# Two weight-row stages, the head scores and the scan outputs of a two-layer mixer moved onto parts of the TensorE array

## What is computed

```
for layer in (0, 1):
    m = silu(c) @ w_mod[layer] + b_mod[layer]        # 6*1024 columns, one row for the latents, one for the context
    z = rms(x) * (1 + m[1]) + m[0]
    layer 0: p = z @ even_w_in                       # 1920 + 1024 columns
             ya = rwkv7_mix(p[:1920])                # a delta-rule scan over time, forward and backward, 8 heads of 64
             yb = rglru_mix(p[1920:])                # gates, a diagonal scan forward and backward
             y  = concat(ya, yb) @ even_w_out
    layer 1: y  = diff_attention(z) @ attn_w_o
    x = x + m[2] * y
    x = x + m[5] * peer_ffn(rms(x) * (1 + m[4]) + m[3])   # product keys, 16 experts per head gathered from HBM

step of the rwkv7 scan, per head:
    sa = state @ kk;  state = state * w - outer(sa, akk) + outer(v, k);  out = state @ r
then out (both directions) is normalised per head, scaled, gated
```

## Time and profile before

| what | value |
|---|---|
| median of 3 runs | 3483.07 us (3481.43 to 3484.12) |
| the profiled execution, its own time | 3485.71 us |
| its span, first to last instruction | 3483.9 us |
| mean granted TensorE clock | 0.933 of full speed |
| TensorE busy | 2802.4 us (80%) |
| VectorE busy | 2254.0 us (65%) |
| ScalarE busy | 701.0 us (20%) |
| POOL busy | 1090.5 us (31%) |

### The profile page before, as it was taken

The page is one execution under the profiler, slowest core; times in us unless marked ns, Lnnn a source line. Parts: engine busy times, 40 slices in busy tenths (PEclk is TensorE's granted clock), DMA queues, the critical chain, the costliest instruction groups (busy, mean ns, idle before and its releaser), DMA issues. The chain is left out here.

```text
span 3483.9 us, 31043 instructions
## 1 busy us (share of the span) xinstructions
PE 2802.4 (80%) x8972; PEld 1425.2 (41%) x8972; DVE 2254.0 (65%) x5072; ACT 701.0 (20%) x1707; POOL 1090.5 (31%) x941
## 2 busy tenths in 40 slices
PE   7697399999967999777787878787696578887777
PEld 1242288888834444322232223232344344432222
DVE  7697423332343767788887888888244367787887
ACT  2112433233102111111111111111104111111111
POOL 0010232122011444444444444444000034444443
PEclk9798699899878999999999999999899899999999
DMA  8552000000014999999999999999300189999998
GB/s 315 185 195 90 33 1 1 1 1 1 1 73 180 362 378 371 413 420 420 420 413 420 421 420 413 418 420 410 148 24 3 74 347 420 420 415 420 421 420 342
DMA packets 133878, 927.54 MB, mean 266 GB/s; under 512 B 16764, under 2 KB 17788, under 8 KB 31380
## 3 DMA queue, kind: packets, MB, share of 16 engines
q0 software_dynamic: 113472, 830.62, 58.1%
q1 hardware_dynamic: 20312, 95.72, 7.4%
HBM read 925.13 MB, written 1.15 MB: 266 GB/s over the span
## 5 line engine op out<-in xcount | busy, mean ns | idle before, releaser
L1370 PE MATMUL psum<-ring,diag 128*128 128x512 f32 x3072 | 1483.8, 622 | 374.7 <-DVE diag L1459 372.7
L1267 POOL DMA_INDIRECT ring<-in_uv,experts x768 | 914.4, 1191 | 1375.4 <-PE psum L1370 1017.9
L1481 DVE CUSTOM_DVE_ANT_0 ring<-ring,hcur 128x1024 f32<-128x1024 f32 x768 | 941.5, 1226 | 261.0 <-DMA ring<-in_uv,experts 240.2
L1370 PEld LDWEIGHTS psum<-ring,diag 128*128 128x128 f32 x3072 | 557.4, 194 | 1276.5 <-DVE diag L1459 799.4
L1301 ACT ACTIVATE gel<-dots 128x1 f32<-128x1 f32 x768 | 143.6, 201 | 1325.4 <-DVE dots L1481 1324.8
L1459 DVE TENSOR_SCALAR diag<-ident,gel,wcur 128x128 f32<-128x128 f32 x768 | 256.8, 345 | 80.2 <-ACT gel L1301 78.0
L385 PE MATMUL psum<-zT,wring 128*128 128x512 f32 x368 | 164.3, 604 | 15.7 <-DMA wring<-in_w_in 15.7
L1015 DVE COPY_PREDICATED T<-level,psum 128x512 f32<-128x512 uint32 x80 | 58.7, 734 | 180.6 <-PE psum L820 180.6
L1350 PE MATMUL psum<-hT,w_q 128*128 128x512 f32 (+3 forms) x512 | 163.1, 473 | 1.4 <-DMA w_q<-in_w_q 1.4
L1543 PE MATMUL psum<-wring,zT 128*128 128x512 f32 x320 | 140.1, 601 | 10.2 <-DMA wring<-in_w_qkv 10.2
L444 DVE SCALAR_TENSOR_TENSOR acc<-wmod,scol,acc 128x512 f32<-128x512 f32 x168 | 126.3, 752 | 6.9 <-ACT acc L411 1.2
(11 more groups left out here) (314 smaller groups left out, 2903.9 us busy)
## 6 DMA issues: line engine op xcount, KB each, us to landing
wring<-in_w_mod SPq DMA_DIRECT2D x12, 2048.0 KB, 9.7
wmod<-in_w_mod POOLq DMA_DIRECT2D x12, 2048.0 KB, 8.4
w_q<-in_w_q SPq DMA_DIRECT2D x32, 512.0 KB
ring<-in_uv,experts POOLq DMA_INDIRECT x768
wring<-in_w_qkv SPq DMA_DIRECT2D x6, 2048.0 KB, 8.4
wring<-in_w_in SPq DMA_DIRECT2D x23, 512.0 KB, 5.0
bc<-modulation_rows SPq DMA_DIRECT2D x14, 512.0 KB, 5.5
w<-in_w_out SPq DMA_DIRECT2D x8, 512.0 KB, 6.2
```

What stands on the lines that cost most here:

```text
L1267: nc.gpsimd.indirect_dma_start(ring[:, s % RING], None, uv, bass.IndirectOffsetOnAxis(ap=experts[:, n, j:j + 1], axis=0)).then_inc(row_in[ ...
L1370: m = nc.tensor.matmul(ps[:, c], diag[:, j % DIAGS], ring[:, j % RING, D + 512 * c:D + 512 * c + 512], start=(first and j == 0), stop=(las ...
L1481: nc.vector.tensor_tensor_reduce(u, u, hcur[:], 1.0, 0.0, ALU.mult, ALU.add, dots[:, j:j + 1]).then_inc(dot_done, 1)
```

## The change

`modulation`: TensorE does all 8 blocks, with 32 stationary columns of which 30 are zero (`scolz`). Block k writes PSUM partitions 32*(k % 4) to 32*(k % 4) + 31. ScalarE evacuates the bank, and one matmul against `sel` adds the four groups.

`project_even`: nothing of layer 1's modulation is left in it, but the loads of the first 4 half chunks (1 MB each), which SP issues last. Layer 1's chunks are done in `rglru` instead, 12 of them spread over its units, in a ring of 4 halves filled by SP.

`rwkv_scan`: `bF` and `kF` hold 64 real rows per head, two heads on the two row halves. Two heads' scores follow each other on the two row halves; all four products of a pair of heads go before the next pair. `R` and the outputs are made with 64 stationary columns and 128 moving ones, even heads into PSUM partitions 0 to 63, odd heads into 64 to 127, so `O` holds them turned (columns of the heads on partitions). `rwkv_finish` turns `O` back with 16 transposes before its first reduction.

```
# modulation
-    for k in range(SPLIT):
-        m = nc.tensor.matmul(ps[0:2, n % BANKS], scol[:, k], wring[:, n % RING, k], start=(k == 0), stop=False)
+    groups(nc, ps[:, n % 2], scolz, wring[:, n % RING], range(KD)).then_inc(part_mm, 1)
...
+def groups(nc, bank, scol, weight, ks):
+    for i, k in enumerate(ks):
+        g = 32 * (k % GROUPS)
+        m = nc.tensor.matmul(bank[g:g + 32], scol[:, k], weight[:, i], start=(k < GROUPS), stop=(k >= KD - GROUPS))
+    return m
...
# project_even
+                for i in range(MOD_RING):
+                    sp.dma_start(wmod[:, i], half_chunk(a, i)).then_inc(wmod_in[i], 16)
...
# rglru: SP, POOL, TensorE, ScalarE, VectorE
+        MOD_AT = lambda u: range(u + (u > 0), u + 2 if u < 7 else MOD_CHUNKS)
+                for i in range(MOD_RING, 2 * MOD_CHUNKS):
+                    sp.wait_ge(part_mm, i - MOD_RING + 1)
+                    sp.dma_start(wmod[:, i % MOD_RING], half_chunk(a, i)).then_inc(wmod_in[i % MOD_RING], 16)
...
+                for n in range(MOD_CHUNKS):
+                    if n >= 2:
+                        pool.wait_ge(row_done, n - 1)
+                    for seg in range(2):
+                        pool.dma_start(brow[seg:seg + 1, n % 2], a["b_mod"][:, 1, n * 512:(n + 1) * 512]).then_inc(b_in[n % 2], 16)
+                    if n >= 2:
+                        pool.dma_start(mod[1, :, (n - 2) * 512:(n - 1) * 512], row[:, n % 2]).then_inc(row_out[n % 2], 16)
...
+                    if u >= 1:
+                        for n in MOD_AT(u - 1):
+                            mod_groups(n)
+                for n in MOD_AT(7):
+                    mod_groups(n)
+                add_groups(MOD_CHUNKS - 1)
...
+                    for n in MOD_AT(u):
+                        act.wait_ge(part_mm, 2 * n + 2)
+                        if n >= 2:
+                            act.wait_ge(sums_mm, n - 1)
+                        nc.scalar.activation(acc[:, n % 2], ps[:, 4 + n % 2], ACT.Copy).then_inc(acc_done, 1)
...
                     if u >= 4:
                         scan(u - 4)
+                    if u >= 1:
+                        for n in MOD_AT(u - 1):
+                            mod_row(n)
                 for u in range(4, 8):
                     scan(u)
+                for n in MOD_AT(7):
+                    mod_row(n)
...
# rwkv_scan
-                        m = nc.tensor.matmul(ps[:, AE_BANKS[i], place(h):place(h) + 256], bF[:, n % 2, h], qrF[:, n % 2, h // 2],
+                        m = nc.tensor.matmul(ps[:, banks[i], place(h):place(h) + 256], side[half(h), n % 2, pair], qrF[half(h), n % 2, pair],
...
-                        m = nc.tensor.matmul(ps[:, 2 + h // 4, (h % 4) * P:(h % 4) * P + P], W[:, (h // 2) * P:(h // 2) * P + P],
-                                             NE[:, h, 1], start=True, stop=True)
+                        m = nc.tensor.matmul(ps[half(h), 2, pair_at(h)], W[:, cols(h)], NE[:, h, 1], start=True, stop=True)
...
+                    for p in range(PAIRS):
+                        two = (2 * p, 2 * p + 1)
+                        for h in two:
+                            nc.tensor.matmul(ps[half(h), 1, pair_at(h)], rkv[:, 2, t, cols(h)], BF[:, h, 1], start=True, stop=False)
+                        for h in two:
+                            nc.tensor.matmul(ps[half(h), 1, pair_at(h)], U[:, cols(h)], NE[:, h, 1], start=False, stop=False)
+                        for h in two:
+                            m = nc.tensor.matmul(ps[half(h), 1, pair_at(h)], S0[half(h), p], RpF[half(h), p], start=False, stop=True)
...
-                        for e in range(2):
-                            rows = slice(HD * e, HD * e + HD)
-                            nc.scalar.activation((bF, kF)[i - 2][rows, b, e:HEADS:2], ps[rows, 4 + i].rearrange("p (a t) -> p a t", a=PAIRS),
-                                                 ACT.Copy).then_inc(tr_done, 1)
+                        nc.scalar.activation((bF, kF)[i - 2][:, b], ps[:, 4 + i].rearrange("p (a t) -> p a t", a=PAIRS),
+                                             ACT.Copy).then_inc(tr_done, 1)
...
# rwkv_finish
+                for t in range(TILES):
+                    for c in range(4):
+                        m = nc.tensor.transpose(ps[:, 4 + t, c * P:(c + 1) * P], O[:, t, c * P:(c + 1) * P], ident[:])
+                    m.then_inc(o_mm, 1)
```

More of the change, by code:

```diff
@@ L31 @@
 MOD_CHUNKS = 6 * D // 512
+GROUPS = 4
+MOD_RING = 4
 WD, AD, GD = range(3)
@@ L166, in _ @@
                 nc.scalar.activation(ctanh[:], cin[:], ACT.Tanh, scale=0.5).then_inc(tanh_done, 1)
-                act.wait_ge(silu_done, 1)
                 for n in range(MOD_CHUNKS):
-                    act.wait_ge(w_in[n % RING], 16 * (n // RING + 1))
+                    act.wait_ge(part_mm, n + 1)
                     if n >= 2:
[L171 to L174, removed]
+                        act.wait_ge(sums_mm, n - 1)
@@ L176, in _ @@
+                    nc.scalar.activation(acc[:, n % 2], ps[:, n % 2], ACT.Copy).then_inc(acc_done, 1)
             @block.vector
             def _(dve):
[L178 to L181, removed]
+                nc.vector.memset(scolz[:], 0.0).then_inc(scol_zero, 1)
                 dve.wait_ge(tanh_done, 1)
-                step(nc.vector.scalar_tensor_tensor(ctanh[:], ctanh[:], 1.0, cin[:], ALU.add, ALU.mult))
@@ L193, in finish @@
                                                    ALU.add, ALU.add).then_inc(row_done, 1)
[L195 to L207, removed]
@@ L774, in _ @@
                     scores_ae(n, 3)
-                    for i in range(4):
-                        if n >= 1 and i == 0:
-                            pe.wait_ge(s_done, n)
-                        if n >= 1 and i == 1:
-                            pe.wait_ge(r_done, n)
-                            pe.wait_ge(o_done, n)
-                        for h in heads_of(i):
-                            m = nc.tensor.matmul(ps[:, BF_BANKS[i], place(h):place(h) + 256], kF[:, b, h], qrF[:, b, h // 2],
-                                                 start=True, stop=True)
-                        m.then_inc(bf_mm, 1)
+                    if n >= 1:
+                        pe.wait_ge(s_done, n)
+                        pe.wait_ge(r_done, n)
+                        pe.wait_ge(o_done, n)
+                    for pair in range(4):
+                        scores(n, kF, BF_BANKS, bf_mm, pair)
                     for lv in range(LEVELS):
@@ L1776, in build @@
         scol = sb(ctx, "scol", [P, KD, 2])
-        ones = sb(ctx, "ones", [P, 2, 2])
-        modulation(nc, a, mod, scol, ones)
+        sel = sb(ctx, "sel", [P, 2])
+        modulation(nc, a, mod, scol, sel)
+        wmod_in = [nc.alloc_semaphore(f"wmod1_in{i}") for i in range(MOD_RING)]
         every, latents = list(range(TILES)), [2, 3]
```

239 lines of the change are left out of this document (99 added, 140 removed).

## The result

The kernel after takes 3374.85 us (median of four runs, 3368.4 to 3377.64), against 3482.25 before (3481.06 to 3484.12): a ratio of 0.9688 [0.9672, 0.9705], faster. The forecast was 3383, from 3358 to 3424. The profiled execution is the fastest of the four, 3368.4 us with a span of 3366.5; against the profiled 3485.7 of before that is -117, and between the medians -107. The stages of one kernel also differ between profiles: the `project_even` of before took 217.3 and 219.0 us where two later runs left it as it was (`scan_only`, `before_ring4`), so up to 5 of its 49.6 us belong to the profile of before.

What follows compares the result with a forecast made beforehand. It took weight arrival to bound `modulation`, TensorE `project_even` and the scan, a ScalarE-VectorE chain `rglru`. Terms -4 (`modulation`), -46 (`project_even`), +31 (`rglru`), -87 (`rwkv_scan`), +3 (`rwkv_finish`) sum to -103 on 3485.7: 3383 us, range 3358 to 3424.

Steps and rivals of the forecast that it cites:

- the sums and `acc` gone from `project_even`: `project_even`: 11 pairs of sum matmuls and all work on `acc` go, -46 us.
- layer 1's chunks paid for in `rglru`: `rglru`: takes over 12 chunks, VectorE's last rows and POOL's stores end it at 89 us, +31.
- outputs at full clock on two column halves: `rwkv_scan`: outputs of a unit take 4.0 us where they took 11.55, -7.5 per unit.
- masks next in line: `rwkv_scan`: once scores shrink to about half, VectorE is late next, with eight masks of 0.67 us.
- rival A: Whole kernel: one record's time per matmul on a part, clock full in the outputs; 3383 us, chance 0.65.
- rival B: Column-group stages: four column groups run at once, `rglru` 80 in place of 89; 3374 us, chance 0.10.
- I take half, 0.435: Matmuls on array parts: 512 columns cost 0.435 us, between 0.87 without overlap and 0.22 with four groups at once.
- the argument from records starting in order: TensorE: the next matmul's first record can join the previous one's second record, but nothing earlier; hence 0.435 us.
- the weights' arrival sets the pace: `modulation`: DMA, 0.98 busy at 380 GB/s, paces the chunks before and after; only the end is won, -4 us.
- the region of the masks: `rwkv_scan`: from output add to first level product, 9.33 us becomes 7.9, -1.5 per unit.
- provided the clock stays full, as it does over all other stretches with 128 or more columns: `rwkv_scan` outputs: condition for 4.0 us a unit; at half clock without overlap 12.8.
- Rival C: `rwkv_scan`: parts overlap but the clock falls in the outputs, 7 to 8 us a unit; 3415 us, chance 0.07.

Runs made afterwards that it cites:

- scan_only: New `rwkv_scan` and `rwkv_finish` put into the kernel before, its three earlier stages left as they were; 3399.98 us, 0.9755.
- before_ring4: The kernel before with four 2 MB weight slots in place of three in the ring of `modulation`; 3479.74 us.
- same_group_next: The kernel after with the two matmuls of each column group next to each other in `modulation`; 3377.33 us.
- rows_between: The kernel after with VectorE making rows 8 to 11 of `rglru` between the last scans, not behind them; 0.9654 of the kernel before.
- filler: The kernel after with one extra unread 512-column matmul per scan unit, ahead of the wait for masks; 3365.58 us, 0.9658.
- both: The kernel after with rows 8 to 11 made between the last scans and the extra unread matmul per scan unit; 3358.23 us, 0.9643.
- after_again: The kernel after, unchanged, measured again on one chip beside later runs; 3368.89 us.
- head_by_head: The kernel after with the scan's outputs made one head at a time instead of grouped in pairs; 3401.17 us.
- scores_one_half: The kernel after with the scan's scores ordered so that two heads of the same row half follow each other; 3377.17 us.
- whole_array: The kernel after with the products of `modulation` and `rglru` on all 128 columns, added up in the same rows; 3456.04 us.

## Why the prediction was right, and which terms were off

Four mechanisms held, each in its stage: the sums and `acc` gone from `project_even`, layer 1's chunks paid for in `rglru`, outputs at full clock on two column halves (but for the last unit), and masks next in line. The price per matmul, which sets rival A apart from rival B, did not. The sum was -103 for a measured -107 between medians and -117 between profiled executions. Stage by stage its misses go both ways: 19 us too little forecast in four stages, 4 us too much in the scan. Its terms:

*The price of a matmul on a part (the step "I take half, 0.435").* This failed: on four column groups it is 0.22 (1.74 / 8), and the argument from records starting in order fell with `same_group_next`. The far lower end of the bounds was the true one, rival B, given 0.10. For pairs of heads the same step was right in size: with two halves, one record's time for each matmul is also what two lines of work fully at once give, so the scan could not tell the two apart. The Trainium skill, page TensorE: Matmul & The Clock Gate, section Part 3: Packing small matmuls — row/col tiling, with 3.07 times for four row tiles, was nearer, and this case's traces go beyond it on four column groups: 6.95 us to 1.74, four times. The term it sizes is `rglru`: 82.0, near rival B's 80 and not 89. Of the 7 us, 5.3 lie before the end of the last scan (70.3 us into the stage, 75.6 forecast) and 1.7 in the tail (11.7 for 13.4). That VectorE, with the last rows behind its scans, and POOL's stores after it end the stage was right (`rows_between`).

*Modulation, -9.0 for -4.* The step "the weights' arrival sets the pace" was wrong for the kernel before (`before_ring4`): it was TensorE and VectorE, 5.15 and 5.18 us a chunk, with a slot freed too late, for an arrival of 4.9. The last chunk is begun 4.6 us earlier in the stage, where about 1.3 was allowed; and from there to the end it is 8.3 us, not 12.6, where the forecast had 3.5 for products that take 1.7.

*Project_even, -49.6 for -46.* The first chunk was there 5.2 us after the stage began, for 6.4; from the first matmul to the last it was 166.0, for 168.3; and 1.4 to the next stage, for 2.0. The size of the removed sums, 18 us of TensorE, was right; the 2.3 us between 166.0 and 168.3 are the records left, 0.429 us each where they took 0.435 beside the sums on VectorE, and why isn't shown. Right as well was that the last sums and stores had ended the stage.

*Rwkv_scan, -83 for -87.* Outputs 3.8 (4.0 forecast), the region of the masks 7.4 (7.9), `R` 1.02 (0.95), the two waits of TensorE for ScalarE gone. By these a unit is 55.8, and four of seven are 1.65 longer, 6.6 us together: the clock falls behind the new wait for masks. The step that failed is "provided the clock stays full, as it does over all other stretches with 128 or more columns": level one has 128 columns. The forecast had named the wait and not what stands behind it. `filler` shows that it is this wait: with 0.9 us of it filled, none of the seven units behind it is long, and none in `both`. Rival C, that the clock falls in the outputs themselves, was wrong for seven units by the window at 1.00, where what it says happened 8 us later; in the last unit it came true, for 1.5 us.

*Rwkv_finish, -0.8 for +3.* The forecast took the transposes at 3.67 us, the row's length at half clock; here they run right behind the scan:

```profile
840.30 1.94 PE L1097 MATMUL psum<-ident,O 128*128 128x128 f32 x16 [1.82 <-PEq L88]
...
842.27 2.29 DVE L1072 TENSOR_REDUCE st<-psum 128x32 f32<-128x2048 f32 x1 [0.90 <-PE psum L1097]
844.60 0.18 DVE L1073 TENSOR_SCALAR st<-st 128x32 f32<-128x32 f32 x1
...
845.14 4.51 POOL L1062 TENSOR_TENSOR KT<-KT,rkv 128x2048 f32<-128x2048 f32 x1 [68.02 <-DMA g_up<-in_g_up]
```

That isn't always so. In `scan_only` the stage is 39.0 us, the rows from the reduction on read:

```profile
874.68 2.29 DVE L1092 TENSOR_REDUCE st<-psum 128x32 f32<-128x2048 f32 x1 [2.49 <-PE psum L1117]
876.06 4.50 POOL L1082 TENSOR_TENSOR KT<-KT,rkv 128x2048 f32<-128x2048 f32 x1 [68.14 <-DMA g_up<-in_g_up]
...
877.01 3.60 DVE L1093 TENSOR_SCALAR st<-st 128x32 f32<-128x32 f32 x1
```

The small instruction on `st` takes 0.18 us if it is done before POOL begins on `KT`, and as long as POOL works if it comes after (3.60, ending with POOL's). Which of the two, the length of the transposes and the arrival of `g_up` decide. The stage was 36.3 or 36.4 where VectorE came first (after, `after_again`, `head_by_head`), 37.4 in `both`, where it came first too but the transposes were slow, and 38.9 to 39.1 where POOL did (`scan_only`, `filler`, `rows_between`, `same_group_next`, `scores_one_half`, `whole_array`). The order was read from the profiles and not set by an edit, so the cause is well supported but not shown by itself.

**Left open.** The medians of the kernel after on two chips, 3374.85 (3368.4 to 3377.64) and 3368.89 (3368.14 to 3370.68), differ by 6 us, and it isn't shown why; the fall of the clock at the last chunk of `modulation` or in the last unit of the scan and the order in `rwkv_finish` can each move it by 1.5 to 2.7 us, but no run separates them. The wider evacuation of `bF` and `kF` and the narrower `R` were not tried alone. Why the clock falls in four units and not in the other three isn't known, nor why it fell in the last unit's outputs in `both` and not in `filler`; no run fills that wait of 1.60 us.

## What to carry to other kernels

Where a matmul uses few output columns, put neighbours on different column groups of the array: four groups of 32 gave the full factor of four in both orders tried, and two halves nearly two, provided that matmuls with the same number of rows stand together. Before work is moved into a stage, look at which queue ends that stage and put the new work ahead of its last serial piece, not behind it. And where a kernel is left with a wait of a microsecond on TensorE, look at the granted clock of the stretch after it: a matmul that nobody reads, put inside the wait, may be worth more than it costs.

## What the hardware showed that was not expected

- Four 32-column groups of float32 run fully at once, 1.74 us for 16 records against 6.95, also when the two matmuls of a group are neighbours. TensorE starts work on a free group past a busy one: four records start in the first 0.1 us in that order too.
- Between 128 and 64 rows the next matmul starts 0.31 to 0.36 us after the last, against 0.27 between two of 128 rows; the cost is per change and not per matmul (0.94 us for one head or for two). The Trainium skill, page TensorEngine Tiling (Array Packing), section Key Properties, says that a change of the mode drains the engine: these gaps agree.
- Behind 1.3 us of idle TensorE and products of 64 columns the granted clock fell, to 0.64 over the next 4.8 us, in four units of seven; in `filler` and `both`, with 0.4 us idle there, it fell in none of fourteen. Behind 1.6 us of idle time and products of 64 columns it was 0.68 over the last unit's outputs.
- A VectorE instruction of 0.18 us took 3.60 while POOL multiplied two operands in SBUF, though the reduction on PSUM beside it kept its 2.29.
